# Two more filling products on TensorE around the ranks of the expert slots, in a two-block transformer kernel

## What is computed

```
g_logits = ht @ w_rg + b_rg                       # 4 groups of experts, one is chosen
e_logits = (ht @ w_re + b_re)[chosen group]       # 8 experts in it, two are chosen
gate     = g_p * softmax(top two of e_logits)
order    = argsort(expert_ids)                    # every (token, expert) pair gets a slot of its expert
y        = (silu(xb @ w_gate[e]) * (xb @ w_up[e])) @ w_down[e]     # for each of the 32 experts e
out      = sum over the two experts of a token of gate * y
```

## Time and profile before

| | |
|---|---|
| median of 3 runs | 697.87 us (697.35 to 697.98) |
| time of the profiled execution | 697.5 us |
| its span | 695.6 us, so 1.9 us of that execution lie outside the span |
| mean granted TensorE clock | 0.989 of full speed |
| PE busy | 670.1 us (96%) |
| PE weight loads busy | 541.2 us (78%) |
| DVE / ACT / POOL busy | 355.5 / 295.0 / 149.1 us |
| read from HBM | 179.70 MB |

### The profile page before, as it was taken

How to read it: one execution, slowest core, us unless ns; L and a number is a source line. 1 busy time by engine, 2 the same in 40 slices (tenths; PEclk the granted TensorE clock), 3 DMA queues, 4 the chain that set the end, 5 groups by cost and what they waited for, 6 DMA issues and landing times.

```text
span 695.6 us, 12108 instructions
## 1 busy us (share of the span) xinstructions
PE 670.1 (96%) x4941; PEld 541.2 (78%) x4941; DVE 355.5 (51%) x579; ACT 295.0 (42%) x486; POOL 149.1 (21%) x148
## 2 busy tenths in 40 slices
PE   6999999999999999999999999998899999999984
PEld 5998886999999999977999999985555555555532
DVE  6359544666666666568555564676222323232313
ACT  5244556454444444455574544334113222322223
POOL 0586865033333333322004000000000000000000
PEclk9999999999999999999999999999789999999999
DMA  8961334555555555542443349888699999999994
GB/s 343 423 255 60 123 106 175 212 193 196 191 193 188 181 181 181 182 179 71 175 164 140 139 165 375 329 339 349 239 412 421 420 420 421 421 420 421 420 421 191
DMA packets 25681, 181.46 MB, mean 261 GB/s; under 512 B 2848, under 2 KB 3104, under 8 KB 4128
## 3 DMA queue, kind: packets, MB, share of 16 engines
q1 hardware_dynamic: 25488, 180.69, 66.6%
q10 hardware_dynamic: 144, 0.07, 0.1%
HBM read 179.70 MB, written 1.05 MB: 260 GB/s over the span
## 4 chain that ended last, share of the span: by engine, by line
PE 85%; DMA 4%; DVE 4%; POOL 2%; ACT 2%; issue 1%; SPq 0%; POOLq 0%; ACTq 0%; DVEq 0%
PE psum L682 50%; PE psum L1287 8%; PE psum L1270 4%; PE psum L1311 4%; PE psum L1294 4%; DMA ring<-units_in 4%; PE psum L1303 4%; PE psum L669 1%; PE psum L645 1%; DVE ffn_w_low L531 1%; DVE arena L2256 1%; PE psum L1028 1%; POOL first_odd L1927 1%; DMA const<-const_in 1%; PE psum L721 1%
## 5 line engine op out<-in xcount | busy, mean ns | idle before, releaser
L531 DVE TENSOR_TENSOR ffn_w_low<-ring,ffn_w_high 128x2048 fp32r<-128x2048 f32 x55 | 131.2, 2386 | 111.0 <-ACT ffn_w_high L526 110.8
L526 ACT ACTIVATE ffn_w_high<-ring 128x2048 fp32r<-128x2048 f32 x56 | 107.4, 1918 | 141.2 <-PE psum L682 141.1
L682 PE MATMUL psum<-ht_high,ffn_w_high 128*128 128x256 f32 x552 | 156.8, 284 | 0.8 <-DVE ffn_w_low L531 0.8
L682 PE MATMUL psum<-ht_low,ffn_w_high 128*128 128x256 f32 x552 | 156.2, 283 | 0.0
L682 PE MATMUL psum<-ht_high,ffn_w_low 128*128 128x256 f32 x552 | 156.2, 283 | 0.0
L682 PEld LDWEIGHTS psum<-ht_high,ffn_w_high 128*128 128x128 f32 x552 | 105.9, 192 | 2.5 <-DVE ffn_w_low L531 1.2
L682 PEld LDWEIGHTS psum<-ht_low,ffn_w_high 128*128 128x128 f32 x552 | 105.9, 192 | 0.3
L682 PEld LDWEIGHTS psum<-ht_high,ffn_w_low 128*128 128x128 f32 x552 | 105.9, 192 | 0.0
L2573 DVE SCALAR_TENSOR_TENSOR weighted<-psum,arena,weighted 128x512 fp32r<-128x512 f32 x31 | 23.3, 751 | 70.3 <-ACT weighted L1813 70.3
L1964 POOL TENSOR_TENSOR arena<-arena 128x512 f32<-128x512 f32 x10 | 28.6, 2864 | 119.3 <-ACT arena L1657 96.9
L1791 ACT ACTIVATE arena<-psum,arena 128x512 f32<-128x512 f32 x32 | 22.0, 687 | 61.1 <-PE psum L1287 53.6
(11 more groups left out here) (398 smaller groups left out, 1296.5 us busy)
## 6 DMA issues: line engine op xcount, KB each, us to landing
ring<-units_in SPq DMA_DIRECT2D x94, 1024.0 KB, 5.0
arena<-units_in SPq DMA_DIRECT2D x29, 1024.0 KB, 22.0
spare_units<-units_in SPq DMA_DIRECT2D x10, 1024.0 KB, 15.6
small_units<-units_in SPq DMA_DIRECT2D x10, 1024.0 KB, 16.9
early_unit<-units_in SPq DMA_DIRECT2D x5, 1024.0 KB, 17.0
HN<-units_in SPq DMA_DIRECT2D x5, 1024.0 KB, 18.7
rows<-units_in SPq DMA_DIRECT2D x4, 1024.0 KB, 17.2
features_unit<-units_in SPq DMA_DIRECT2D x4, 1024.0 KB, 20.9
```

Of the source, the lines that this page charges most:

```text
L526: nc.scalar.activation(parts_slot(n)[0], w, ACT.Copy).then_inc(hi_ready, 1)
L531: nc.vector.tensor_tensor(l, ring[:, n % RING, :], h.bitcast(fp32), SUB).then_inc(lo_ready, 1)
L682: last = mm(o, l[a], r[b], start=start and (a, b) == pairs[0], stop=stop and (a, b) == pairs[-1])
```

## The change

Two calls are added on TensorE, one on each side of the five rank products. The first is a filling product of 256 columns behind the one of 512 columns and ahead of the wait for `m_ready`. The second is a filling product of 384 columns behind the rank products and ahead of the wait for `onehot_ready`. Both write bank 2 of PSUM, and both take the same constant as the one before.

```diff
@@ -1254,6 +1254,7 @@
             residual(0)
             residual(1).then_inc(x_summed, 1)
             stay_busy(1, 2, c_("iota"))
+            stay_busy(1, 2, c_("iota"), 256)
             pe.wait_ge(m_ready, 1)
             every, before = rank_terms[:, 0:P], rank_terms[:, P:2 * P]
@@ -1261,6 +1262,7 @@
                     last = mm(psum[:, 3, n * EXPERTS:(n + 1) * EXPERTS], l, chosen[:, tt, :], start=(l, tt) == terms[0],
                               stop=(l, tt) == terms[-1])
             last.then_inc(rank_done, 1)
+            stay_busy(1, 2, c_("iota"), 384)
 
             def gather(bank, features, slots=BATCH * CH):
```

## The result

The changed kernel takes 693.89 us in the median of 5 runs (693.18 to 695.39). The kernel before takes 697.98 us beside it (697.35 to 698.98). The ratio is 0.9941, with a 95% interval of 0.9925 to 0.9957. That is 4.1 us faster (3.0 to 5.2 by the interval), where 2.8 us were forecast, and it lies 0.1 us under the range of 694.0 to 697.2. The profiled execution took 693.89 us, 3.6 us less than the one before (697.5), with a span of 692.1.

What follows compares the result with a forecast made beforehand. The stream of expert units was taken to set the end. Gathers 1.95 us faster plus first unit 0.8 us gave 2.75, say 2.8 us, so 697.87 us became 695.1 us, with a range of 694.0 to 697.2.

Steps and rivals of the forecast that it cites:

- What bounds the kernel.: Expert stage: the stream of expert units sets the end; a TensorE gain counts only as far as it starts that stream earlier.
- The first and the second filler, both hidden.: Around the rank products: 0.44 and 0.66 us of filler cost nothing, hidden by waits for DVE.
- What the two do to the clock.: Gathers and first four units: with both fillers, TensorE's clock holds at 1.00 instead of falling to 0.50.
- The gathers at full clock, the first unit.: Before the first issue: gathers end 1.95 us earlier, first unit saves 0.8 us, moving the issue from 494.65 to about 491.9.
- To the end: From first issue to last landing: the stream starts 2.8 us earlier at unchanged bytes and rate, so the end moves 2.8 us.
- It costs nothing at the end: Between table and first down product: the second clock fall stays, some 3.4 us earlier, without the queue running empty.
- a bound of 3.4 us: Upper limit of the gain, if all TensorE's lead reaches the end because the stream's slow first microseconds run better.
- the narrow gathers bring the clock down: Rival at the gathers: the clock falls all the same and the fillers buy nothing, 697.9 us; chance 0.11.
- The shortened stretch: Rival: the clock falls among the gathers but recovers before the first unit, which ends 0.85 us sooner, 697.0 us; chance 0.05.
- The fall in the tail: Rival near the end: the clock is at half from about 680 on, costing 5.3 us, 700.4 us in all; chance 0.04.

Runs made afterwards that it cites:

- e8: The changed kernel with the first expert unit moved ahead of the third group of gathers: median 695.02 us, ratio 0.9964 to the kernel before.
- The third series: Here the changed kernel run again without an edit, beside the kernel before: median 694.52 us against 697.81, ratio 0.9963.
- e5: The changed kernel with a filler of 320 columns added on TensorE between the first and second expert unit: median 695.24 us, ratio 0.9958.
- e6: The changed kernel with the second filler of 768 columns instead of 384: median 694.46 us, ratio 0.9957 to the kernel before.
- e4: The changed kernel with fillers of 640 and 256 columns added between the table and the first down product: median 693.11 us, ratio 0.9934.

## Why the prediction was wrong by its size and right by its mechanism

*What bounds the kernel.* Right for the two kernels compared: the last unit is taken up 0.04 us behind its landing in both. A gain on TensorE counts as far as it brings the stream forward: with the fillers at the table, 3 us of lead on TensorE became 0.8 us at the last landing of a profiled execution. There TensorE itself was the later one at the very end, by 0.36 us.

*The first and the second filler, both hidden.* Right: a pause of 0.44 us was left, and the gathers began at 487.04.

*What the two do to the clock.* Right for both together, in both traces of the changed kernel; the other 14 executions fit by their times. It wasn't said that each is needed. The first alone leaves the median as it was, and the second alone gives the short time in 12 of 22 executions.

*The gathers at full clock, the first unit.* Right: 491.89 for the first issue, 491.9 forecast.

*"To the end: the stream starts 2.8 us earlier, has the same bytes and the same rate."* This step failed. Its term is the 2.8 us from the first issue to the end, and the profiled pair measures 3.49 us: 2.76 at the first issue and 0.73 inside the stream. The rate at the start isn't given. It depends on how far ahead of need the second and the later units are asked for, and those were held up by the low clock more than the first: the second issue moved by 3.32 us (496.07 to 492.75), and the end by 3.49. The unit placed early (e8) shows it from the other side. The prediction had the figure, 344 GB/s in the slow start, and used it only for a bound of 3.4 us. The term of the sum should have been 3.3 to 3.5 us, which gives 694.4 to 694.6 us, inside the range. That the second issue's lead sets the pace at the first unit's end is shown, over fourteen traces. How much of the 0.73 us comes from there isn't, since the rest of the stream varies as much: from the ninth landing to the last it took 162.7 to 164.2 us.

*"It costs nothing at the end"*, of the second fall. Wrong as a rule, and put at nothing on a count that was too short; filling it is worth 1.4 us between medians of one series. Its length doesn't explain the 0.73 us, since both kernels of the pair have this fall for 6.83 us. The argument counted five issues, and the thin place is behind them, at the sixth and seventh. Where the fall lasts 10.24 us the stream drops to 246 GB/s.

*The remaining 0.5 us* between the profiled gain of 3.6 us and the 4.1 us of the medians is within the spread, and lies with the kernel before, whose profiled execution was 0.5 us under its median. The third series gave 3.3 us, and single executions of the changed kernel lie 3.4 us apart. The range was built on three runs of the kernel before that agreed within 0.6 us; 93 more lie between 692.85 and 700.60. A range of 694.0 at its low end left no room for that. That the median fell 0.1 us under the range and not inside is chance: the changed kernel's second median, 694.52, is inside.

*The rivals.* That the narrow gathers bring the clock down whatever stands before them is ruled out, since they ran at 1.00. So the Trainium skill's account (TensorE: Matmul & The Clock Gate, on oscillation in real kernels), idle gaps longer than any here, doesn't cover this case: filling pauses of 0.88 and 0.78 us held the clock in both traces. The shortened stretch wasn't seen for the first fall; for the second it was, 3.41 us in e5 and e6. The fall in the tail did happen, in e4 from 671.06 to 674.48 and in e6 from 670.45 to 673.86. The stretch in e6:

```profile
670.45:673.86 3.41, 3.08 (x14) 1.22 (x16) 0.35 (x1) 0.69 (x1) 0.00 (x0) 0.50 1.00 418
```

Those executions took 693.17 and 693.11 us, among the fastest. It was shorter than the rival supposed, and it lay at 671, not from 680 on, so most of it was made up before the last landing. Not all: TensorE found no more landing to wait for from 670.7 on and took the last unit up 0.36 us behind its landing in e4 and 0.26 us in e6, where the twelve other traces have 0.04 to 0.05. The mechanism of that rival is real, at some 0.3 us.

## What to carry to other kernels

Short pauses with narrow products between them can cost more than they last, if the clock falls behind them; a product that nobody reads, put where the engine would wait anyway, is free as long as it ends before the wait does. Where a stream of transfers sets the end, look at its first handful of issues and at the places where the next one is asked for only just ahead of need, and not only at the first. And time such a kernel in many executions: three that agree can all be of one kind.

## What the runs showed of the hardware that wasn't expected

Transfers have a price for coming late that shows before the queue is empty: with the next unit of 1 MB issued 2.5 us ahead of the end of the one in flight, single packets took up to 1.3 us instead of 0.31, and the stream ran at 348 instead of 420 GB/s for 4 us. With 2.95 us or more no such packets came at the end of the first unit.

The same kernel has its falls at other places and for other lengths from one execution to the next. The second low stretch of the changed kernel was at 498.83 to 505.66 in one profiled execution and at 496.82 to 507.06 in the other, though the work ahead of both was the same within 0.6 us. Of the kernel before, about one execution in eight took 693 us; what its clock did there was not profiled, but its mean over the span was 0.992 to 0.995 in those, against 0.982 to 0.989 in the others. The changed kernel has 0.989 to 0.994, so this mean alone doesn't tell the cases apart.

A filler isn't always as cheap as its columns. Between other products of 512 columns, 256 more cost the 0.44 us that was worked out. Put between two units, whose products use 32 columns of weights each, 320 cost 0.87 us instead of 0.55. Why wasn't tried.
